# Turning the normed queries and keys of the first attention: 32 turns on TensorE replaced by 32x32 block turns on VectorE and 32 block moves on ScalarE

## The reference

```
q_a, f_a, i_a, g_a, q_b, k_b, v_b, gate_logits = jnp.split(h @ w_in, split_pts, axis=-1)
gates = sigmoid(gate_logits + b_gate);  gate_a, gate_b = split(gates, 2)
y_a = hgrn2_mixer(q_a, f_a, i_a, g_a, ...)
qh = head_rms_norm(heads(q_b), q_gain)     # per token and head: t * rsqrt(mean(t*t) + EPS) * gain
kh = head_rms_norm(heads(k_b), k_gain)
scores = einsum('bhnqd,bhnkd->bhnqk', qh, k_band) * scale + bias
o = softmax(scores) @ v_band
merged = gate_a * (y_a @ w_proj_a) + gate_b * (y_b @ w_proj_b)
```

## Time and profile before

| | |
|---|---|
| time, median of 3 runs | 2562.52 us (2562.3 to 2562.54) |
| profiled execution, its own time | 2565.37 us |
| profiled execution, span | 2563.6 us |
| PE busy | 2546.2 us |
| DVE busy | 1871.1 us |
| ACT busy | 1306.2 us |
| granted TensorE clock, mean | 0.999 |

### The profile page before, as it was taken

One profiled execution on the slowest core, in us unless ns is written; L12 is line 12 of the kernel. 1 busy time (PEld: TensorE's weight loads), 2 busy tenths in 40 slices (PEclk: granted clock), 3 DMA queues, 4 the chain that ended last, 5 costly groups with the idle time before them and its releaser, 6 DMA issues.

```text
span 2563.6 us, 33953 instructions
## 1 busy us (share of the span) xinstructions
PE 2546.2 (99%) x11732; PEld 2117.6 (83%) x11732; DVE 1871.1 (73%) x2440; ACT 1306.2 (51%) x1667; POOL 18.7 (1%) x28
## 2 busy tenths in 40 slices
PE   9999999999999999999999999999999999999998
PEld 7888888888888888888888788888888888888887
DVE  6787768666567777777776776885698777777786
ACT  6545456554455555555555545555644444444443
POOL 0000000000000000000000000000000000000000
PEclk9999999999999999999999999999999999999999
DMA  8876767676568877788777587774477776677665
GB/s 308 271 256 210 232 214 239 201 234 220 188 195 261 257 259 252 256 257 259 255 258 257 169 248 234 222 221 149 156 234 229 219 218 218 218 216 219 212 217 181
DMA packets 281444, 584.30 MB, mean 228 GB/s; under 512 B 17968, under 2 KB 28384, under 8 KB 280432
## 3 DMA queue, kind: packets, MB, share of 16 engines
q1 hardware_dynamic: 279376, 574.25, 70.5%
q0 software_dynamic: 1952, 8.49, 1.1%
HBM read 580.54 MB, written 2.13 MB: 227 GB/s over the span
## 4 chain that ended last, share of the span: by engine, by line
PE 94%; DMA 2%; DVE 2%; ACT 1%; issue 0%; SPq 0%; DVEq 0%; ACTq 0%
PE acc L1306 82%; PE W L1306 10%; DMA raw<-in_w_in 2%; DVE wlo L1806 1%; PE W L1530 0%; ACT whi L634 0%; PE W L1388 0%; PE acc L1661 0%; DVE arena L1871 0%; DVE hHL L1878 0%; PE W L1498 0%; DVE raw L1819 0%; PE acc L1388 0%; DVE crow L1953 0%; DVE arena L2641 0%
## 5 line engine op out<-in xcount | busy, mean ns | idle before, releaser
L1806 DVE TENSOR_TENSOR wlo<-raw,whi 128x1024 fp32r<-128x1024 f32 x888 | 1081.7, 1223 | 643.4 <-ACT whi L634 640.2
L634 ACT ACTIVATE whi<-raw 128x1024 fp32r<-128x1024 f32 x888 | 937.1, 1059 | 1069.4 <-PE acc L1306 800.1
L1306 PE MATMUL acc<-whi,hHL 128*128 128x512 f32 x4992 | 1246.2, 391 | 2.3 <-ACT whi L634 1.8
L1306 PEld LDWEIGHTS acc<-whi,hHL 128*128 128x128 f32 x4992 | 932.2, 188 | 196.3 <-issue 2.5
L1306 PE MATMUL acc<-wlo,hHL 128*128 128x512 f32 x2496 | 668.9, 389 | 0.0
L1306 PEld LDWEIGHTS acc<-wlo,hHL 128*128 128x128 f32 x2496 | 468.5, 188 | 98.3 <-DVE wlo L1806 0.4
L1819 DVE CUSTOM_DVE_ANT_0 raw<-raw,crow 128x1024 f32<-128x1024 f32 x192 | 233.8, 1218 | 3.0 <-DMA raw<-in_w_ada_t 2.8
L1306 PE MATMUL acc<-whi,yH 128*128 128x512 f32 x768 | 209.6, 395 | 2.8 <-issue 2.8
L1306 PE MATMUL acc<-whi,yL 128*128 128x512 f32 x768 | 206.3, 390 | 0.0
L1306 PE MATMUL acc<-wlo,yH 128*128 128x512 f32 x768 | 205.5, 389 | 0.0
L1306 PEld LDWEIGHTS acc<-whi,yH 128*128 128x128 f32 x768 | 143.8, 188 | 33.3 <-issue 3.9
(11 more groups left out here) (222 smaller groups left out, 1115.7 us busy)
## 6 DMA issues: line engine op xcount, KB each, us to landing
raw<-in_w_in SPq DMA_DIRECT2D x264, 512.0 KB, 4.7
raw<-in_w_ada_t SPq DMA_DIRECT2D x192, 512.0 KB, 4.8
raw<-in_w_ffn_in SPq DMA_DIRECT2D x176, 512.0 KB, 4.6
raw<-in_w_up SPq DMA_DIRECT2D x128, 512.0 KB, 4.2
raw<-in_w_down SPq DMA_DIRECT2D x128, 512.0 KB, 4.5
raw<-in_w_ffn_out SPq DMA_DIRECT2D x88, 512.0 KB, 4.8
raw<-in_w_out SPq DMA_DIRECT2D x32, 512.0 KB, 4.3
raw<-in_w_o SPq DMA_DIRECT2D x32, 512.0 KB, 4.2
```

The lines of the kernel that those rows point to most:

```text
L634: act.activation(whi[:, v], raw[:, s], ACT.Copy).then_inc(S("w_hi"), 1)
L1306: return pe.matmul(o, l, r, start=start, stop=stop, skip_group_check=True)
L1806: dve.tensor_tensor(wlo[:, v], raw[:, s], whi[:, v].bitcast(F32), ALU.subtract)\
```

## The change

For queries and keys (k = 1 and 2) TensorE's 16 turns each and ScalarE's one copy each are gone. VectorE, right behind the multiplication in `head_apply`, waits for its own result and then runs two transposes of 128x1024 each, which turn each 32x32 block in its place and write the blocks ordered by bank into a free buffer (`ST` for the queries, `dec` for the keys). ScalarE then moves the blocks: 16 activations of 32 partitions x 512 for each k, from partitions 32i to partitions 32j, each scaled by the gain. They are put in fours behind each of the eight units of the fourth gate group (`head_shift(k, i)`: u = 0 to 3 queries, 4 to 7 keys). The turn for k = 0 stays.

```diff
-            def head_copy(k):
+            def head_shift(k, i):
                 def run():
                     x, g = ((qb, q_scale), (kb, V("k_gain")))[k - 1]
-                    act.wait_ge(S("hn_turn"), k + 1)
-                    act.activation(backward(x) if k == 1 else x.rearrange("p (j t) -> p j t", t=P),
-                                   Wf.rearrange("p (j t) -> p j t", t=P), ACT.Identity, scale=g).then_inc(S("hn_done"), 1)
+                    dst = backward(x) if k == 1 else x.rearrange("p (j t) -> p j t", t=P)
+                    if i == 0:
+                        act.wait_ge(S("hn_bank"), k)
+                    for j in range(4):
+                        src = head_banked[k - 1][32 * i:32 * i + 32, j * 512:(j + 1) * 512].rearrange("p (k c) -> p k c", c=32)
+                        ins = act.activation(dst[32 * j:32 * j + 32, :, 32 * i:32 * i + 32], src, ACT.Identity,
+                                             scale=g[32 * j:32 * j + 32])
+                    if i == 3:
+                        ins.then_inc(S("hn_done"), 1)
...
-            group(hooks={1: head_copy(1), 5: head_copy(2), 6: gate_sig(2, M)})
+            hooks = {u: head_shift(1 + u // 4, u % 4) for u in range(8)}
+            hooks[6] = lambda: (head_shift(2, 2)(), gate_sig(2, M)())
+            group(hooks=hooks)
...
-            group(8, hH, hL, (("vb_in", 2),), hooks={1: hgrn_out, 7: head_turn(0)})
-            group(8, hH, hL, (("gate_lin", 1),), hooks={5: head_turn(1)})
-            group(8, hH, hL, (("gate_lin", 2),), hooks={1: head_turn(2), 7: slot(0, 0, N_B)})
+            group(8, hH, hL, (("vb_in", 2),), hooks={1: hgrn_out, 7: head_turn()})
+            group(8, hH, hL, (("gate_lin", 1),))
+            group(8, hH, hL, (("gate_lin", 2),), hooks={7: slot(0, 0, N_B)})
...
                     dve.tensor_tensor(x, x, rr[:, 1].unsqueeze(2).to_broadcast([P, 2 * H, P]), ALU.mult)\
                        .then_inc(S("hn_in"), 1)
+                    if k:
+                        dve.wait_ge(S("hn_in"), k + 1)
+                        dst = head_banked[k - 1].rearrange("p (j h t c) -> p t j h c", j=4, h=H, t=TT)
+                        for t in range(TT):
+                            src = tokens((qb, kb)[k - 1])[:, t].rearrange("p (h j d) -> p j h d", h=H, j=4)
+                            ins = dve.transpose(dst[:, t], src)
+                        ins.then_inc(S("hn_bank"), 1)
```

More of the change, by code:

```diff
@@ L296, in tokens @@
             return ap.rearrange("p (t n) -> p t n", t=TT)
+        head_banked = [ST, dec]
         def by_bank(ap):
@@ L1485, in fq_turn, with head_turn @@
                 return run
-            def head_turn(k):
+            def head_turn():
                 def run():
[L1490 to L1495, removed]
+                    pe.wait_ge(S("hn_in"), 1)
+                    x = tokens(ob)
                     for h in range(H):
```

## The result

| | before | after |
|---|---|---|
| time, median | 2562.54 us (5 runs, 2562.3 to 2565.03) | 2576.53 us (5 runs, 2575.62 to 2577.7) |
| ratio | | 1.0052, 95% interval 1.0041 to 1.0062 |
| profiled execution, own time | 2565.37 us | 2577.43 us |
| profiled execution, span | 2563.6 us | 2575.6 us |

The change makes the kernel slower by 14.0 us in the medians and by 12.1 us in the two profiled executions. The forecast was 2574.3 us, +11.8, with a range up to 2577.0. The changed kernel again in a later session had 2575.37 us against 2564.54 of the kernel before beside it, +10.8 (ratio 1.0044, 1.0030 to 1.0057). So the difference of the medians differs by some 3 us between the two sessions.

The account below looks back on a forecast made before the run. TensorE was taken as the bound; after the change ScalarE's list of root, splits, 32 moves and sigmoid decides p0. Its +11.8 us, with TensorE's saved 3.58 not taken off again, gave 2574.3 us, range 2569.0 to 2577.0.

Parts of the forecast that it names:

- The bound and the lead: TensorE bounds the kernel; ScalarE's split is ahead of it by only 0.6 us at d0, 4.5 at p0.
- The saved work: On TensorE the two removed turns, 1.78 and 1.80 us, take off 3.58 us, 0.14% of the time.
- rival 3: All new work hidden and TensorE keeps its step: p0 at 430.98, 2558.9 us; chance 0.02.
- VectorE's turns: On VectorE ahead of c6's and d1's `lo`: 1.20 us each, 2.33 a pair, costing more than they give back.
- its list of waits: TensorE's new waits, 15.4 us: c6 1.4, d0 2.1, d1 2.7, d3 to d6 4.6, d7 3.6, p0 and scores the rest.
- The floor of +2.7 us without moves: Even with free moves, VectorE's late d1 brings p0 at 437.3, 2.7 us later than 434.56.
- ScalarE's moves: On ScalarE from the root to p0: 32 moves of 0.72 us without overlap, 23.04 us, the large term.
- The choice between ends: Move spacing on ScalarE: 0.585 us at the lower bound, as full-width activations, 0.755 at the upper, for strided access.
- Rival 1: ScalarE's moves overlap like full-width activations: 32 of about 0.60 us, +8.0, 2570.5 us; chance 0.25.
- The sum: ScalarE's list from the root at 410.98 ends at 446.37, so p0 comes 11.8 us later than 434.56.
- the high end of the range: Moves at 0.755 us, turns at 2.76 a pair, up to 1.0 for the next group: +14.3, taken as 2577.0 us.
- rival 4: TensorE's granted clock falls in the new waits; one or two units at 1.2 GHz give +13 to +16, about 2577; chance 0.05.

Follow-up runs that it names:

- e4: Changed kernel without VectorE's four block turns and without 30 of the 32 ScalarE moves: 2562.36 us, ratio 0.9992 to the kernel before.
- e1: Changed kernel without 30 of the 32 block moves on ScalarE, block turns kept: 2566.92 us, ratio 1.0012 to the kernel before.
- e5: Changed kernel with each move writing the same 32 partitions that it reads: 2573.99 us, ratio 1.0038 to the kernel before.
- e6: Changed kernel with 8 full-width activations of 128x512, no shift of partitions, in place of the 32 moves: 2566.91 us, ratio 1.0011 to the kernel before.
- e2: Changed kernel with every fourth block move left out, 24 of 32 kept: 2570.56 us, ratio 1.0027 to the kernel before.
- e11: Changed kernel with small matmuls on TensorE in the waits ahead of d0 and d7: 2576.23 us, ratio 1.0044 to the kernel before.
- e12: The changed kernel unaltered, measured again in a later session: 2575.37 us, ratio 1.0044 to the kernel before.
- e7: Changed kernel with moves that copy without the gain's scale from memory (Copy for Identity): 2574.51 us, ratio 1.0039 to the kernel before.
- e9: Changed kernel with all 32 scaled moves on GpSimd in place of ScalarE: 2600.19 us, ratio 1.0136 to the kernel before.
- e10: Changed kernel with the queries' 16 moves on GpSimd, the keys' 16 on ScalarE behind d2 to d5: 2570.71 us, ratio 1.0025.
- e8: Changed kernel with 20 small products on TensorE between c7 and d0: 2577.06 us, ratio 1.0045 to the kernel before.
- e3: Changed kernel without VectorE's four block turns, ScalarE's moves kept: 2575.02 us, ratio 1.0044 to the kernel before.

## Why the prediction was right

**The bound and the lead.** The step that decided was to read how far ScalarE was ahead at d0 (0.6 us) and p0 (4.5 us), not how much of its time was free overall. ScalarE is busy for 51% of the span before and after.

**The saved work.** 3.58 us were forecast. Even without any new work 1.67 of them don't come back, most of them waited away at d0 (e4). In rival 3 I left this out: its 2558.9 us were never to be had; e4 shows 1.91 of the 3.58.

**VectorE's turns.** 1.20 us forecast, 1.223 measured; a pair 2.33 and 2.37. Waits forecast 1.4 at c6, 2.1 at d0, measured 1.28 and 1.93. The prediction lets PE want d1's `wlo` near 418.0, which is a slip: from its own start of d0 it is 412.25 + 2.72 + 1.81 = 416.8, and its list of waits goes by that, with 2.7 for d1. Measured, d0 and d1 together take 2.76 us more than two units (411.03 to 419.23). The floor of +2.7 us without moves was +2.84 in e1.

**ScalarE's moves.** 0.72 us from start to start forecast, 0.73 measured; the duration is 0.720 in the mean. The choice between ends was whether moves overlap. L1001's pairs said no and were right. By the figures of the Trainium skill's page "ScalarE: Activation LUTs" (What ACT_TABLE_LOAD costs) an estimate is 0.613 us from start to start. That is what e5 and e6 measure, 0.61, where activations stay on their partitions; where they go from one set of partitions to another the trace shows 0.73. So in these runs its overlap of about 93 ns holds for the first kind alone. Rival 1 would have been right for moves that stay on their partitions.

**The sum.** p0 was to come 11.8 us later; it came 11.94 later, and the window from d0 to p0, forecast at about 34 us, has 34.12. The step from split to split was forecast at 3.97 and is 4.02. From start to start PE loses 4.68 us ahead of d3 to d6 and 3.52 ahead of d7, where 4.6 and 3.6 were forecast. So the mechanism held term by term. The loss in the next group, which only the high end of the range had (up to 1.0), is 0.5 us and belongs in the sum. Two things are luck: the profiled execution came out so near to the sum (2577.43 us against 2577.2) because its differences elsewhere in the program nearly cancelled, and the median of +14.0, 2.2 above the forecast, stayed within the range by 0.5. The +10.8 of the later session lies below the forecast; what makes the difference between the sessions is open.

**The clock** (rival 4). It fell, against a chance of 0.05: from 411 to 416 the granted clock was 0.66 of full speed in the mean, a mix of 2.4 and 1.2 GHz:

```profile
411.00:416.00 5.00, 4.97 (x15) 3.99 (x16) 4.93 (x5) 4.91 (x7) 0.00 (x0) 0.66 0.39 115
```

PE had waited 1.28 us at c6 and 1.93 ahead of d0. The same two waits were followed by no fall in e1, e2, e5 and e6, so whether it falls differs between executions. It cost nothing here, since d1 waits for `wlo` anyway (e11 against e12). The price in the prediction, one or two units at half speed on the path, fits only a fall at d7, where 0.8 to 2.4 us were lost.

## What to carry to other kernels

Price work that is moved to an engine off the critical path by the lead of that engine at the place, split by split, and not by its share of free time. On ScalarE the count of instructions decides: 32 activations of 32x512 cost as much each as 128x512 did, and where they go between partitions they don't overlap either, so 23 us stood in for two copies of 1.95. A transpose in blocks saves TensorE's turn, but not the move of the blocks, and that is the larger part.

## What the runs showed of the hardware

Activations of 32x512 start 0.73 us apart in fours of which three write other partitions than they read, and 0.61 apart when all write the same ones, with durations of 0.72 and 0.71; activations of 128x512 are 0.61 apart (e6). A scale from a column of memory costs 0.09 us per activation (e7, and the 0.093 of the earlier trace rows). The same move takes 1.6 to 2.3 us on GpSimd, and some of VectorE's splits beside it take 1.4 to 1.6 us in place of 1.22. TensorE's granted clock fell after waits of 1 to 3 us near each other, at d0 in four profiles (after, e7, e9, e12), at d2 in one (e10) and at d7 in three (e5, e7, e8). It fell in no such place in e1, e2, e3 and e6, which have such waits as well, so these runs show no rule for it. At d0 and d2 other waits hide it. At d7 it cost some 0.8 us in e8, 1.2 in e7 and 2.4 in e5 (estimates: p0's start there against the end of p0's split and the 0.14 us that lie between the two in the changed kernel). So the place where it falls decides what it costs.
